# Turning attention weights by DVE blocks and DRAM instead of TensorE, in a hybrid encoder on one core

## What is computed

```python
def diff_attention(q, k, v, lam):              # second branch, 4 heads
    s = jnp.einsum('bhtqd,bhtkd->bhtqk', qblk, k) * scale
    p = jax.nn.softmax(s, axis=-1)
    w = p[:, :, 0] - lam * p[:, :, 1]
    return jnp.einsum('bhqk,bhke->bhqe', w, v)
...
    for window, dil in DIL_PATTERNS:           # third branch, 8 heads of 64
        o_g, lse_g = dilated_window_attention(qc, kc, vc, dil, window // (2 * dil))
    wts = jax.nn.softmax(jnp.stack(lses, axis=0), axis=0)
    o_c = jnp.einsum('gbhs,gbhsd->bhsd', wts, jnp.stack(outs, axis=0))
...
    y_b = rms_norm(o_b) * (1.0 - lam_init) * jax.nn.silu(b_g)
    y_c = o_c * jax.nn.silu(c_g)
```

## Time and profile before

| | us |
|---|---|
| median of 3 runs | 1239.95 (1239.26 to 1241.86) |
| the profiled execution | 1237.68 |
| its span, first to last instruction | 1235.9 |
| TensorE busy | 1210.9 (98%) |
| DVE, ACT, POOL busy | 695.7, 441.9, 832.1 |

### The profile page before, as it was taken

How to read it: one execution, slowest core, us unless ns; L and a number is a source line. 1 busy time by engine, 2 the same in 40 slices (tenths; PEclk the granted TensorE clock), 3 DMA queues, 4 the chain that set the end, 5 groups by cost and what they waited for, 6 DMA issues and landing times.

```text
span 1235.9 us, 17632 instructions
## 1 busy us (share of the span) xinstructions
PE 1210.9 (98%) x5840; PEld 984.2 (80%) x5840; DVE 695.7 (56%) x1037; ACT 441.9 (36%) x799; POOL 832.1 (67%) x595
## 2 busy tenths in 40 slices
PE   7999999999999999999999999999999999999995
PEld 5877888788878887787888778887887798777884
DVE  6686327532753385677658841583247335648842
ACT  6425523542454235100253453145324532450012
POOL 5787377638762976677749753885488548757881
PEclk9999999999999999999999999999999999999998
DMA  6333233323332333374244222523252314336611
GB/s 241 103 119 113 94 103 109 106 94 113 100 104 93 119 102 129 125 256 154 90 155 145 86 105 77 170 79 107 73 153 90 116 56 148 102 107 232 204 69 68
DMA packets 52079, 148.62 MB, mean 120 GB/s; under 512 B 6848, under 2 KB 8384, under 8 KB 51648
## 3 DMA queue, kind: packets, MB, share of 16 engines
q1 hardware_dynamic: 29088, 103.04, 24.0%
q10 hardware_dynamic: 22944, 44.98, 12.0%
HBM read 114.45 MB, written 16.78 MB: 106 GB/s over the span
## 4 chain that ended last, share of the span: by engine, by line
PE 93%; DVE 3%; DMA 1%; ACT 1%; ACTq 1%; issue 1%; POOLq 0%; POOL 0%; DVEq 0%
PE proj L1098 53%; PE proj L1202 10%; PE turn L1337 4%; PE turn L1263 3%; PE score L1337 3%; PE score L1255 3%; PE score L1256 2%; PE mbank L1271 2%; PE obank L1271 2%; PE mbank L1337 2%; PE obank L1337 2%; PE proj L1116 1%; PE obank L1290 1%; DMA big<-big 1%; DVE yl L1033 1%; PE mbank L1090 1%
## 5 line engine op out<-in xcount | busy, mean ns | idle before, releaser
L426 POOL TENSOR_TENSOR wl<-raw_w,wh 128x512 fp32r<-128x512 f32 x352 | 503.9, 1452 | 31.7 <-POOL wh L417 31.7
L417 POOL TENSOR_SCALAR wh<-raw_w 128x1024 fp32r<-128x1024 f32 x176 | 215.4, 1224 | 284.6 <-issue 101.9
L1098 PE MATMUL proj<-hh,wh 128*128 128x512 f32 x1024 | 405.6, 396 | 0.5 <-DVE big L1060 0.5
L1098 PE MATMUL proj<-hh,wl 128*128 128x512 f32 x1024 | 400.5, 391 | 0.0
L1098 PE MATMUL proj<-hl,wh 128*128 128x512 f32 x1024 | 399.5, 390 | 0.0
L1098 PEld LDWEIGHTS proj<-hh,wl 128*128 128x128 f32 x1024 | 192.2, 188 | 41.8
L1098 PEld LDWEIGHTS proj<-hh,wh 128*128 128x128 f32 x1024 | 192.4, 188 | 41.0 <-issue 1.3
L1098 PEld LDWEIGHTS proj<-hl,wh 128*128 128x128 f32 x1024 | 192.5, 188 | 39.2
L536 ACT ACTIVATE six<-big 128x512 f32<-128x512 f32 x24 | 15.0, 626 | 202.9 <-DVE big L1060 202.9
L949 DVE CUSTOM_DVE_ANT_0 six<-score,lmask 128x512 f32<-128x512 f32 x64 | 43.2, 684 | 66.3 <-PE score L1256 66.3
L907 DVE TENSOR_TENSOR group<-big,group 128x512 f32<-128x512 f32 x24 | 37.5, 1613 | 71.7 <-ACT big L633 71.4
(11 more groups left out here) (205 smaller groups left out, 1886.8 us busy)
## 6 DMA issues: line engine op xcount, KB each, us to landing
raw_w<-weights SPq DMA_DIRECT2D x175, 512.0 KB, 3.3
gate_scratch<-gstage ACTq DMA_DIRECT2D x48, 256.0 KB, 2.0
six<-gate_scratch ACTq DMA_DIRECT2D x16, 768.0 KB, 5.4
big<-big ACTq DMA_DIRECT2D x64, 128.0 KB, 4.2
yh<-yh ACTq DMA_DIRECT2D x64, 128.0 KB, 2.4
big<-x_t SPq DMA_DIRECT2D x4, 512.0 KB, 6.6
big<-x_t SPq DMA_DIRECT2D x1, 2048.0 KB, 8.9
x_scratch<-big SPq DMA_DIRECT2D x1, 2048.0 KB, 7.3
```

The source lines that it names most:

```text
L417: pool.tensor_scalar(wh[:, slot, :, :], src, 1.0, 1.0, ALU.mult, ALU.mult).then_inc(pool_high.sem, 1)
L426: ins = pool.tensor_tensor(wl[:, slot, half, :], src[:, half, :], wh[:, slot, half, :].bitcast(F32), ALU.subtract)
L1098: last = pe.matmul(dst, a[:, slot, k, :], b[:, k, :], start=(k == 0 and a is wh and b is hh), stop=(k == KT - 1 and a is wl))
```

## The change

Units 0 to 7 (the second branch, and now all four query blocks of the third's first head) go another way:

- DVE inverts the sums (inverse), ACT scales the map in place in probs (scale), and for units 0 to 3 DVE adds the second map.
- DVE turns the 32x32 blocks with one transposing instruction into w (turn_32). w is laid out so that two units, a *pair*, interleave in it; the pair uses both slots.
- SP writes the pair to a DRAM scratch, one DMA for each band of 32 partitions (send, runs of 64 floats), waits for that, and reads it back with blocks in their places (bring, four DMAs, runs of 256 floats) into wt or wt1. The four sends and four brings of a group stand in SP's stream between weight loads 12 and 16 and behind them.
- The order of the third branch's maps is now head by head. Units 8 to 11 (its second head) are still turned by TensorE.
- TensorE's order of fillers is rewritten, the second branch's values come after scores(5), and three elementwise operations address tokens in 128-wide pieces, since the pairs interleave tokens.

```diff
+VIA = list(range(0,8))
+BY_PE = [u for u in range(12) if u not in VIA]
...
+            def send(G, m):
+
+                sp.wait_ge(*turned_32.at(G, 2 * m + 2))
+                for a in range(4):
+                    sp.dma_start(turned_d[m, :, :, a, :], w[32 * a:32 * a + 32, :, :].rearrange("i n s -> i (n s)").rearrange(
+                        "i (x j) -> i x j", j=64)).then_inc(sent.sem, 16)
+
+            def bring(G, m):
+
+                u = VIA[2 * m]
+                if u == 4:
+                    sp.wait_ge(*c_parts.at(G, 1))
+                    apart(sp)
+                sp.wait_ge(*sent.at(G, 64 * (m + 1)))
+                k, q = (0 if u >= 4 else QB), 2 * P * (u % 4 // 2)
+                for c in range(4):
+                    sp.dma_start(big[32 * c:32 * c + 32, k:k + QB, q:q + 2 * P], turned_d[m, :, QB * c:QB * c + QB, :, :].rearrange(
+                        "i x a j -> i x (a j)")).then_inc(back.sem, 16)
...
+                        if j == 12:
+                            send(L * NG + i, 0)
+                            bring(L * NG + i, 0)
+                        if j == 13:
+                            send(L * NG + i, 1)
+                        if j == 14:
+                            bring(L * NG + i, 1)
+                        if j == 15:
+                            send(L * NG + i, 2)
+                    bring(L * NG + i, 2)
+                    send(L * NG + i, 3)
+                    bring(L * NG + i, 3)
...
+                    def scale(u):
+
+                        j = 2 * u if u < 4 else u + 4
+                        act.wait_ge(*rs_ready.at(G, VIA.index(u) + 1))
+                        act.activation(probs[:, j % 4, :], probs[:, j % 4, :], ACT.Copy, scale=rs[:, j:j + 1]).then_inc(scaled.sem, 1)
...
+                    def turn_32(u):
+                        j = 2 * u if u < 4 else u + 4
+                        dve.wait_ge(*scaled.at(G, VIA.index(u) + 1))
+                        if u < 4:
+                            dve.wait_ge(*rs_ready.at(G, VIA.index(u) + 1))
+                            grp.did(dve.scalar_tensor_tensor(probs[:, j % 4, :], probs[:, (j + 1) % 4, :], rs[:, j + 1:j + 2], probs[:, j % 4, :],
+                                                             ALU.mult, ALU.add))
+                            grp.last()
+                        if u >= 2:
+                            dve.wait_ge(*w_free(G, u))
+                        dve.transpose(by_quarter(w[:, :, :], u % 2), probs[:, j % 4, :].rearrange("p (k c j) -> p k c j", k=QB, c=4)).then_inc(turned_32.sem, 1)
...
-                    turn_weights(0)
                     for u in range(1, 4):
                         scores(u + 1)
                         fill(5)
                         if u == 1:
                             mean_of(mbank, 1)
...
+                    fill(3)
+                    scores(5)
+                    fill(4)
+                    pe.wait_ge(*back.at(G, 2 * 64))
+                    values(out_done, (obank[:, :], slice(P, 2 * P), wt))
+                    fill(3)
+                    scores(6)
+                    fill(4)
+                    pe.wait_ge(*y_read.at(G, 2))
+                    mean_of(obank, 2)
+                    fill(3)
+                    scores(7)
```

More of the change, by code:

```diff
@@ L137, in low_of, with steps_of_weights, build @@
     return 6 * n + 4 + head
+def steps_of_weights():
+    return sum(2 if u in VIA else 3 for u in range(4)) + sum(1 for u in range(4, 12) if u not in VIA)
 def unit_of(j):
     return j // 2 if j < 8 else j - 4
-def build(nc, x_d, w_d, par_d, up_d, gain_d, cos_d, sin_d, lmask_d, cmask_d, gmask_d, ident_d, out_d, gate_d, xkeep_d):
+def build(nc, x_d, w_d, par_d, up_d, gain_d, cos_d, sin_d, lmask_d, cmask_d, gmask_d, ident_d, out_d, gate_d, xkeep_d, turned_d):
     with ExitStack() as ctx:
@@ L309, in build @@
         pool_high = sig("pool_high", ROWS_LAYER)
+        sent = sig("sent", PAIRS * 64)
+        back = sig("back", PAIRS * 64)
         swapped = sig("swapped", 2 * 64)
@@ L727, in group @@
                     exp(1)
+                    scale(0)
                     for u in range(4):
@@ L756, in group @@
                             act.wait_ge(*out_done.at(G, 4))
-                            grp.did(act.activation(rr[:, 1, :], obank[:, :], ACT.Ln, bias=cst[:, 0:1]))
+                            for b in range(QB):
+                                ins = act.activation(tokens(rr[:, 1, :], b), by_token(obank, b), ACT.Ln, bias=cst[:, 0:1])
+                            grp.did(ins)
                             grp.last()
@@ L944, in row_max @@
                         else:
[L945 removed]
+                            b = j % 4
                             if j >= 10:
@@ L994, in group @@
                     row_max(3)
-                    weights(0)
+                    inverse(0)
+                    turn_32(0)
                     for u in range(1, 4):
-                        weights(u)
+                        inverse(u)
                         if u == 1:
@@ L1264, in turn_weights, with values @@
                         last.then_inc(turn_done.sem, 1)
-                    def values(ready, done, *products):
-                        pe.wait_ge(*wt_ready.at(G, ready))
+                    def values(done, *products):
                         for k in range(QB):
@@ L1298, in group @@
                             mean_of(mbank, 1)
-                        turn_weights(u)
-                    fill(3)
-                    values(4, out_done, (obank[:, :], slice(P, 2 * P), wt))
-                    for u in range(4, 10):
-                        if u % 2 == 0:
-                            scores(u // 2 + 3)
-                        fill(3 if u in (5, 7) else 4)
-                        turn_weights(u)
-                        if u == 5:
-                            pe.wait_ge(*y_read.at(G, 2))
-                            mean_of(obank, 2)
+                    fill(3)
[10 more added lines that the diff above has]
+                    scores(7)
+                    for u in range(8, 10):
+                        fill(4)
+                        turn_weights(u)
                     fill(4)
```

127 lines of the change are left out of this document (89 added, 38 removed).

## The result

The changed kernel takes 1319.63 us (median of 4 runs, 1317.54 to 1322.45) against 1239.66 for the kernel before in the same session: a ratio of 1.064, 95% interval 1.062 to 1.067. It is slower, as forecast, but by 80 us where the forecast said 39, though the time lies within the range (1238 to 1325).

What follows compares the result with a forecast made beforehand. TensorE, busy 98% of the span, bounds the kernel; per group 8.55 us of new waits less 3.44 of transposes and 0.25 of old wait give +4.86, eight groups +38.9 on 1239.95: 1279 us, range 1238 to 1325.

Steps and rivals of the forecast that it cites:

- transposes removed: TensorE loses 256 of 384 transposes, 64 batches at 0.43 us: 27.5 us saved, 3.44 a group.
- (a): On ACT's queue scale(0) stands ahead of exp(2), so TensorE waits 0.9 us a group at scores(2).
- (b): The same 1.65 us delay runs on through ACT and DVE; TensorE waits 1.8 us a group at scores(3).
- (c): Low-part copies are issued behind scale(2) on ACT's queue, so TensorE waits 0.75 us a group at scores(4).
- (d) values of the second branch: Exchange through DRAM, sends 4.8 us and brings 4.6: TensorE waits 4.1 us a group at these values.
- (d) weights(8): weights(8) on DVE needs its slot back from send(3), so TensorE waits 1.0 us a group.
- granted clock: TensorE's clock left at 0.996 over the span, priced at nothing, since new pauses are 4 us at most.
- rival of 1.3 us: DVE's block transposes take 1.3 us instead of 0.7: +3.0 us a group, 1303 us; chance 0.08.
- each us comes back three times: Each extra us in a send returns three times a group: at turn_32(2), the values and weights(8).
- rival of short runs: 256-byte runs make a send 6.5 us: +5.1 us more a group, about 1320 us; chance 0.20.
- faster: Exchange hidden, ACT and DVE catch up; waits about 2.1 us, a group gains 1.6: 1227 us; chance 0.12.
- (e): SP's later weight loads, the last of a group by some 4 us, cost TensorE nothing.

Runs made afterwards that it cites:

- x8: Changed kernel with only units 4 to 7 sent through DRAM, own buffers, read back early, second branch by TensorE; 1225.59 us, 0.989 of the kernel before.
- x3: Changed kernel with all sends and brings and their waits left out; 1241.07 us, 1.001 of the kernel before.
- x12: x8 with the second branch's values also waiting for two chained tiny DMAs, started once unit 3 is turned; 1239.59 us, 1.0007.
- x15: x8 with four chained tiny DMAs ahead of the second branch's values and 22 unread matmuls ahead of that wait; 1269.59 us, 1.024.
- x16: Changed kernel with separate buffers, so pairs no longer share the two slots of w; 1313.79 us, 1.060 of the kernel before.
- x7: Changed kernel with sends writing 4 KB runs instead of 256 bytes, brings unchanged, so weights land in wrong places; 1295.28 us, 1.046.
- x9: x8 with the second branch's values also waiting for one tiny DMA issued after scores(4); made no pause; 1224.89 us.
- x11: x8 with the second branch's values also waiting for three chained tiny DMAs started after scores(4); made no pause; 1226.19 us.
- x18: x16 with scale(0) moved behind exp(3) and the low-part copies ahead of scale(2) on ACT's queue; 1295.82 us, 1.045.
- x1: Changed kernel with 18 unread matmuls ahead of TensorE's wait for the second branch's values; 1305.21 us, 1.052 of the kernel before.
- x2: x1 with 10 more unread matmuls ahead of the wait for the copies before scores(4); 1303.0 us.
- x13: x8 with the second branch's values also waiting for three chained tiny DMAs, started once unit 3 is turned; 1269.07 us, 1.023.

## Why the forecast was right in sign and wrong in size

Per group, against the steps of the prediction:

| step | forecast | measured | from |
|---|---|---|---|
| transposes removed | -3.44 | not refuted: 13.3 us saved by x8 for 13.8 expected | x8 |
| (a) scores(2) waits for exp | 0.9 | 0.73 | third group |
| (b) scores(3) waits for exp | 1.8 | 1.54 | third group |
| (c) copies of the low parts | 0.75 | 20.4 / 8 = 2.55 | waits |
| (d) values of the second branch | 4.1 | 38.2 / 8 = 4.8 (4.21 in the third group; both ends 4 us late, see below) | waits |
| (d) weights(8) | 1.0 | 2.5 / 8 = 0.3 | waits |
| granted clock | 0 | 32 / 8 = 4.0 that no wait explains; 25.2 / 8 = 3.15 of it against x3 | span, busy times |

The spans differ by 82.0 us where 38.9 were forecast. The 43 us between are 32 of slower work, 14.4 at the copies and 5.4 at the values more, 3.4 at exps and 5.5 at weights(8) less, and 0.5 by old waits that stayed.

**The sign** was right for the stated reason. TensorE was full, every engine behind it was just in time, and the waits (a), (b) and (d) stood at the places named, within 1 us each. For (d) the size was luck. The prediction has scores(3) at 341.05, the trace at 360.65, 19.6 later; counted from there, TensorE stands at the values at 360.2 (379.80), not 356.3, and the data is there at 364.4 (384.01), not 360.4. TensorE was 3.9 us late by the copies and the slower work, the data 4.0 by sends of 5.64 and 6.68 us (4.8 taken) and a bring of 5.4 (4.6 taken), and the two misses cancelled in their difference. The block transpose was right too: 711 ns (0.7 was taken), even beside POOL, so the rival of 1.3 us falls. The cause is one of order and distance: with the exchange left out the change is worth nothing (x3), and half of it, placed where the exchange has time, is worth 1.1% (x8).

**The step that failed** is the last of the sum: "granted clock, 0.996 over the span, I leave as it is: the new pauses are 4 us at most". That put a term at nothing which was worth 3 to 4 us a group; the reason given, "4 us at most", stands on none of its rows, which show no TensorE behind a pause. x12 to x15 show the term alone: 2.2 us behind a pause of 3.3, 2.6 behind one of 4.8, and nothing left in TensorE's busy time when the pause is filled. In the changed kernel the group has two such places, behind the copies and behind the values; filling the second gave 14.4 us back. Not all of the 32 us is clock. x3, at clock 0.997, also spans 1239.1 us where its waits less its savings give 1233.4 (1235.9 - 27.5 - 1.8 + 26.8), 5.7 us over 25 pauses. For the same 5584 matmuls TensorE is busy 1214.6 us in the changed kernel and 1189.4 in x3: 25.2 us, 3.15 a group, go with the pauses that the exchange makes.

**Two smaller misses** came on top. Term (c) was priced as if the copies landed in 2.4 us as in the earlier trace rows. send(0) runs at the same time (362.48 to 368.12, the copies issued at 363.39), and they landed in 3.3 and 3.9. The pair of copies issued at 355.99, before any send of the group, landed in 2.3 and 2.4. The prediction had both start times and did not put them side by side. x3 has 1.06 instead of 2.55: 1.5 us a group for a collision. And a send was 5.9 instead of 4.8. Yet "each us comes back three times" did not hold: weights(8) hardly waited, and DVE's wait for send(0) hid behind scores(4) (x16: 6 us for taking away 71 us of DVE's waits). x7 puts a price on it: 1.6 us less in a send gave 24.3 us, 1.9 a group for each us, clock included. At that price the 1.1 us by which a send was longer than forecast comes to about 17 us (an estimate), mostly the same us as those of the clock, the copies and the values above. The rival of short runs gave 1320, which is the time measured; it is not what happened, for its 6.5 us sends and its 3-fold return are not in the trace.

One sum of the prediction does not follow from its own times. In the rival *faster* 0.4 us stays at the values; with sends of 2.9 and a bring of 3.6 the data would be there at 355.9, before TensorE at 356.3, so nothing stays and the case ends at 1224, not 1227. The forecast does not use it.

Step (e), SP's late loads at nothing, held: no wait of TensorE for split weights appears, and x9 to x11 held SP's stream up without cost. x16 to x18 show a limit of the prediction's picture: between scores(4) and the values lies one chain (copies, scores, maxima, sum, transpose, send, bring), and taking a wait out of its early part moves TensorE up as well, so that the last wait grows.

What stays open: of the 25 us, x1 took back 14.5 (busy 1233.1 less 33.0 for its 144 unread matmuls, against 1214.6) and x2 another 4.7, and for the last 6 no run shows the place, nor for the 6 that x3 has already; and what of term (c)'s collision is the sends' bytes and what is their 256-byte runs (x7, with long runs, still has 16.8 us of that wait and a landing of 3.1).

## What to carry to other kernels

Where TensorE is full, price an idle stretch of it twice: its length, and the slower work behind it; pauses of 3.3 and 4.8 us cost two thirds and half as much again here, one of 1.6 us nothing more. A long transfer chain is free where its result is used much later and it shares no buffer, and not where the next step needs it: so move only the part whose consumer is far away. Before taking landing times from a trace, look up which other transfers will run in the same microseconds after the change.

## What the runs showed of the hardware that was not expected

- Granted clock of TensorE after one idle stretch: 1.00 after 1.65 us (x12), 0.50 for the next 5.5 us after 3.15 (x13); eight value matmuls took 6.5 us instead of 3.7. After 2.48 us, in the changed kernel, it still read 1.00 in the first microsecond of new work and 0.50 two microseconds on.
- DVE's transposition of the 32x32 blocks of a 128x512 fp32 map: 705 to 715 ns in all 48 written to group in x16, while the two-input sum just before it ranged from 0.74 to 2.08 us in the changed kernel's third group.
- Writes of 128 KB in runs of 256 bytes against 4 KB: four take 5.9 us instead of 4.3 until the DMA that waits for them is issued (mean of the third group's four), and SP needs 2.8 us instead of 1.75 to issue the first four.
- Two copies of 128 KB on ACT's queue landed in 3.3 and 3.9 us beside SP's short writes, and in 2.3 and 2.4 with none beside them, in the same group.
